# A decoder step on one core: VectorE takes each latent page apart four half pages ahead of its key products, in place of five

## The reference, cut to what matters

```
def page_block(phys):
    kn, kr, v = mla_keys(cache_l[phys], w_uk, w_uv, k_norm_nope)   # kn = rms_norm(c @ w_uk), 8 heads of 128
    return partial_softmax(mla_scores(qn, qr, kn, kr), v)
m_p, l_p, a_p = lax.map(page_block, page_table.T)
```

## Time and profile before

| | us |
|---|---|
| median of 3 runs | 1407.22 (1404.19 to 1407.71) |
| the profiled execution | 1408.25 |
| its span, first to last instruction | 1406.5 |
| PE busy in the span | 1381.6 (98%) |
| DVE, ACT, POOL busy | 1015.2, 857.7, 292.9 |
| page loop, about 95 to 1065 on PE | 970 for 128 pages |

### The profile page before, as it was taken

One profiled execution on the slowest core, in us unless ns is written; L12 is line 12 of the kernel. 1 busy time (PEld: TensorE's weight loads), 2 busy tenths in 40 slices (PEclk: granted clock), 3 DMA queues, 4 the chain that ended last, 5 costly groups with the idle time before them and its releaser, 6 DMA issues.

```text
span 1406.5 us, 30025 instructions
## 1 busy us (share of the span) xinstructions
PE 1381.6 (98%) x9428; PEld 1168.5 (83%) x9428; DVE 1015.2 (72%) x3674; ACT 857.7 (61%) x2780; POOL 292.9 (21%) x339
## 2 busy tenths in 40 slices
PE   9999999999999999999999999999999999999998
PEld 7877887887778777778877888778778999999998
DVE  5766667788777886877887777778765567777543
ACT  5445788687666686575866666865783453444332
POOL 3012312222422222331322322322331000000000
PEclk9999999999999999999999999999999999999999
DMA  9442326753445544356543564444564565555551
GB/s 282 126 119 51 80 48 147 166 123 76 95 111 146 119 114 80 72 127 158 124 99 84 113 130 99 86 98 87 113 165 160 169 240 164 167 180 180 181 182 58
DMA packets 282890, 180.05 MB, mean 128 GB/s; under 512 B 183072, under 2 KB 229696, under 8 KB 282728
## 3 DMA queue, kind: packets, MB, share of 16 engines
q1 hardware_dynamic: 282418, 177.86, 49.5%
q10 hardware_dynamic: 318, 0.33, 0.1%
HBM read 134.32 MB, written 6.77 MB: 100 GB/s over the span
## 4 chain that ended last, share of the span: by engine, by line
PE 81%; DVE 7%; ACT 6%; issue 3%; SPq 2%; DMA 1%; POOL 0%; DVEq 0%; ACTq 0%
PE ps L2067 14%; PE ps L2069 13%; PE ps L2068 13%; PE ps L2471 6%; PE ps L2472 6%; PE ps L2473 6%; PE ps L2089 2%; ACT ksq L895 2%; PE ps L2142 2%; PE ps L2419 2%; PE ps L2420 2%; PE ps L2421 2%; PE ps L2143 2%; PE ps L2144 2%; DVE prod L1285 1%
## 5 line engine op out<-in xcount | busy, mean ns | idle before, releaser
L2067 PE MATMUL ps<-ukh,cTh 128*128 128x512 f32 x1024 | 416.6, 407 | 8.8 <-DVE sparts L1285 7.1
L895 ACT ACTIVATE ksq<-ps 128x128 f32<-128x128 f32 x1024 | 268.1, 277 | 235.8 <-PE ps L2069 235.1
L2068 PE MATMUL ps<-ukl,cTh 128*128 128x512 f32 x1024 | 400.9, 392 | 0.0
L2069 PE MATMUL ps<-ukh,cTl 128*128 128x512 f32 x1024 | 400.9, 392 | 0.0
L1285 DVE CUSTOM_DVE_ANT_0 prod<-ps,qb 128x128 f32<-128x128 f32 x1024 | 234.0, 284 | 23.8 <-ACT ksq L895 19.3
L2067 PEld LDWEIGHTS ps<-ukh,cTh 128*128 128x128 f32 x1024 | 193.3, 189 | 63.5 <-issue 25.2
L2069 PEld LDWEIGHTS ps<-ukh,cTl 128*128 128x128 f32 x1024 | 192.8, 188 | 42.7
L2068 PEld LDWEIGHTS ps<-ukl,cTh 128*128 128x128 f32 x1024 | 193.2, 189 | 34.1
L747 POOL TENSOR_TENSOR rk<-kss,mhalf 128x8 f32<-128x8 f32 x128 | 217.5, 1699 | 10.7
L895 ACT ACTIVATION_READ_ACCUMULATOR ksq<-ps 128x1 f32 x1024 | 212.6, 208 | 0.0
L882 ACT ACTIVATE cTr<-turned 128x1024 uint16<-128x1024 uint16 x126 | 174.8, 1387 | 2.4 <-DMA turned<-planes 2.3
(11 more groups left out here) (504 smaller groups left out, 2701.1 us busy)
## 6 DMA issues: line engine op xcount, KB each, us to landing
clat<-cache_mla SPq DMA_DIRECT2D x128, 256.0 KB, 2.6
wraw<-w_in SPq DMA_DIRECT2D x16, 1024.0 KB, 5.1
wraw<-w_up SPq DMA_DIRECT2D x16, 1024.0 KB, 5.4
wraw<-w_down SPq DMA_DIRECT2D x16, 1024.0 KB, 5.0
braw<-w_in SPq DMA_DIRECT2D x24, 512.0 KB, 4.5
crope<-cache_mla SPq DMA_DIRECT2D x128, 32.0 KB, 2.4
qb<-scratch SPq DMA_DIRECT2D x16, 256.0 KB, 3.7
sst<-state_gdn SPq DMA_DIRECT2D x32, 128.0 KB, 3.1
```

Source lines behind the costliest of these rows:

```text
L895: i = nc.scalar.activation(ksq[m % 3], ps[:, k % 3, P * h:P * h + P], ACT.Square, accum_out=kss[:, n // 4 % 2, n % 4, h0 + h:h0 + h + 1]). ...
L2067: mm(out, cTh[:, n % 2, c], ukh[:, c, cols], start=c == 0, stop=False)
L2068: mm(out, cTh[:, n % 2, c], ukl[:, c, cols], start=False, stop=False)
L2069: i = mm(out, cTl[:, n % 2, c], ukh[:, c, cols], start=False, stop=c == 3)
```

## The change

DVE's `split_planes` moves from behind `beside(2n+1)` to behind `split_lo(n+1)`, and takes page `n+2` in place of `n+3` there. A page is so taken apart one iteration later less the steps between the two places: four half pages ahead of its key products, where it was five. No instruction is added or taken out.

```
                     scored(n - 1, 1)
                 if n + 1 < NT:
                     split_lo(n + 1)
+                if n and n + 2 < NT:
+                    split_planes(n + 2)
                 if t == 1 and g >= 1:
                     scaled(g - 1)
...
                 beside(2 * n + 1)
-                if n + 3 < NT:
-                    split_planes(n + 3)
                 if n:
                     scored(n, 0)
```

## The result

The changed kernel takes **1468.52 us** (median of 4 runs, 1463.84 to 1470.35) where the kernel before takes 1407.47 (1404.19 to 1407.81): a ratio of 1.0435, with a 95% interval of 1.0415 to 1.0455. It is slower by 61 us. The direction was forecast, but the size was not: 16.6 us were forecast, and the range ended at 1438. The profiled execution took 1463.84 us, with a span of 1462.1 us. So what the trace shows (1462.1 - 1406.5 = 55.6 us more) is a little less than the difference of the medians.

The account below looks back on a forecast made before the run. PE, busy 98% of the span, was taken as the bound. Terms of 9.5 + 3.1 + 5.0 - 1.0 = +16.6 us gave 1423.8 us; forecast 1413 to 1432 (67%), range 1409 to 1438.

Parts of the forecast that it names:

- The ring: Page loop: landed, cTr, cTh, cTl, copy, issue on SP, landed; no page follows its predecessor in less than 6.7 us.
- four such stretches: Around pages 26, 52, 67 and 102, ACT works without pause and a late landing delays everything; 1.25 us each.
- The closing pages: Pages 119 to 127 ran at 5.84 us each, under the ring's length: +9.5 us, bounds +3.1 and 18.5.
- The projections: Pairs 1 and 3: the copy now precedes bwl, which ends 0.61 us later: +3.1 us, bounds 0 and 6.1.
- The other tight pages: Four loop stretches where ACT has no pause and late landings delay everything: +5 us, bounds 0 and 12.
- the forecast's last sentence: Wrong if closing pages stay under 6 us, landings get much quicker, or PE's waits grow at unnamed places.
- The gain: DVE's waits for a landing before the copy vanish, mostly without cost to PE before: -1.0 us, bounds 0 and -3.
- Covered: Rival: ACT's waits for PE in the loop absorb late landings; 1407 to 1411 us; 14%.
- faster: Rival: DVE scores banks sooner, so PE's 7.1 us of waits for them go; 1401 to 1403 us; 4%.
- SP snowballs: Rival: 25 group loads on SP's queue each add 1.3 us to the ring; 1433 to 1445 us; 15%.

Follow-up runs that it names:

- the loads two and two: The kernel before, SP's four page loads of a group split into two and two around its first page's transposition: 1406.37 us, ratio 1.0003.
- opening the ring: The changed kernel with the copy two pages ahead put in front of the next page's low half: 1424.28 us; 1431.18 on another chip.
- the kernel without a ring: The changed kernel copying three pages ahead (six half pages), each group's first-page copy left at its old place: 1419.01 us, ratio 1.0091.
- The six-half-page run: The changed kernel with its copy at the new place taking the page three ahead instead of two: 1445.97 us, ratio 1.0279.

## Why the prediction was right in its sign and wrong in its size

**The ring** was right, with its length. The transpositions of the changed kernel stand 6.66 us apart where nothing else is in the way (499.11 to 505.77), and 6.7 was worked out. That shortening it, lengthening it and opening it all move the time, and that the same edits move the kernel before little or not at all, is shown by the runs.

**The step that failed** is: "in long pages the ring has time to spare, and it gives back lateness there", together with "I see some four such stretches", 1.25 us each. The ring was set against the loop's mean of 7.6 us a page. But the pages are not turned at their mean. In the kernel before, one in four comes 9.5 us after its predecessor, and the other three come at 6.9 to make up for it. SP's loads in between are half of the reason: with the loads two and two it is still 8.6, against 7.2. The rest is probably DVE's softmax steps (`scaled`, `probabilities`, `accumulate`), which it does once a group between these two copies; no run shows it. Against 6.7 the three pages have 0.2 us each to spare. Even that is too much: 6.7 was reckoned with the median landing, 3.2 us, but the landings of the changed kernel have a mean of 3.39, with one in four over 3.5 and the longest 6.3, and wherever the ring is the bound it pays them. With the mean it is 6.9, and nothing is left. The issues could no longer bunch as before (6.9 became 7.5), and the mean went from 7.57 to 8.02 us: (1047.2 - 101.1)/125 by the earlier trace rows, against (1103.5 - 101.1)/125 by

```profile
L534 SPq DMA_TRANSPOSE turned<-planes x126: 1232/1237/2617, 101.1 to 1103.5; - x126
```

0.45 us for each of 125 steps, 56 us in all. Splitting the loads gives 24 us back and opening the ring 37 to 44, which bears this out. With both, 55 of the 61 us are gone.

Where PE lost them is to be seen page by page, from the start of each page's first product against the kernel before. It is 0.5 us late at page 26, 4.7 at 28, 5.8 at 42, 13.1 at 48, 18.9 at 54, 29.3 at 93, 34.1 at 99, 39.7 at 119 and 55.6 at 127 (1113.05 against 1057.47). The four stretches that were named (26 to 28, 50 to 54, 67 to 68, 102 to 104) make 12.1 us of it, where 5 were put. From 42 to 48 and from 93 to 99, where pairs 1 and 3 make their projections, it is 12.1 as well. These are pages of 9 to 10 us, the long ones in which lateness was to be given back. 3.4 of these 12.1 us are the clock (the two stretches from 436.80 and 471.00).

**The closing pages** were forecast at +9.5 us (3.1 to 18.5). `cTl` of page 119, 120 and 127 in the changed kernel:

```profile
1047.86 0.68 DVE L1273 TENSOR_TENSOR cTl<-cTr,cTh 128x512 fp32r<-128x512 f32 x1
...
1050.32 0.69 DVE L1261 COPY planes<-clat 128x1024 uint16<-128x1024 uint16 x1 [1.78 <-DMA crope<-cache_mla]
...
1058.94 0.69 DVE L1273 TENSOR_TENSOR cTl<-cTr,cTh 128x512 fp32r<-128x512 f32 x1 [5.24 <-ACT cTh L885]
...
1108.88 0.69 DVE L1273 TENSOR_TENSOR cTl<-cTr,cTh 128x512 fp32r<-128x512 f32 x1
```

From 119 to 127 it is 61.0 us where 46.75 were the earlier trace rows, +14.3. From first product to first product on PE, as the term was reckoned, it is +15.8 (64.0 where 48.1 were), within the bounds. Nothing behind the loop gave it back, as forecast. The seven rounds took 49.9 us, and 48.9 were worked out (7 x 6.7 and 1.95). Most of the rest is the step to page 120, 11.1 us, since the copy for page 120 came at 1050.32 only, after 1.78 us of waiting for the page itself, and SP's state writes and page loads held the transposition until 1053.28. But page 119 was already 1047.86 - 1008.15 = 39.7 us late, where the other terms gave 7.1. Nearly all that was missed arose in the body of the loop.

**The projections** (+3.1) hold for what they priced: the wait for `bwl` went from 3.2 to 6.2 us, and the kernel without a ring has it too. The pages around them lost more, as said.

**The other tight pages** (+5, bounds 0 to 12) is the term that failed in size: what the terms for the projections, the tight pages and the gain had to cover came to 39.7 us. Two parts of it were counted nowhere. One is the pair steps held up behind `cTl`. I had put the late landing on ACT and on the page alone. On DVE it stops everything behind it, and PE's new waits for `qkv`, `X_`, `oT`, `Xc` and their like are what the forecast's last sentence named as the sign that it would be wrong. The other is the clock: 9.4 us of PE time at 1.2 GHz, of which the sum had none.

**The gain** (-1.0): DVE's wait for landings before the copy is gone, as forecast, and no gain is to be seen. It turned up one instruction earlier: `cTl`'s wait grew by 79.5 us.

**The rivals.** "Covered" and "faster" are out. "SP snowballs" had the right mechanism (the loads meet a ring with no spare time) and was still too small with its 12 to 20 us, since it too let the projection pages clear the lateness. The six-half-page run shows a further bound that I hadn't seen: the copy can't come much earlier either, as the page isn't there yet. The old place lies between the two.

No version here beats the kernel before. The kernel before with its loads two and two is the same (ratio 1.0003).

Left open: how the 12.5 us of the run without a ring divide between the steps held up by the copy and DVE's longer waits for the planes to be read.

## What to carry to other kernels

When a change closes a ring, set the ring's length against the shortest spacing that the loop needs to catch up, not against its mean: one slow step in four, here a group's first page with SP's loads ahead of it, uses up what the mean seems to leave. Reckon the ring with the mean of its transfers, not with their median, where they have a long tail. Then list what is queued behind each wait of the ring on its in-order engine, work of other streams included, as that is where the bound engine starts to wait. A producer has a place that is too early (its input hasn't arrived) and one that is too late (its own successor waits); swapping two neighbouring instructions across the wait was worth 40 us here.

## What the runs showed of the hardware

- A transposing DMA of 128x1024 two-byte numbers lands 3.2 us after its issue at the median (mean 3.39 in the changed kernel and 3.55 in the kernel before), one of 128x512 2.4 us, and SP is held for 1.24 and 1.19 us by them: half the bytes save a quarter of the time to landing and almost nothing of the issue.
- In the changed kernel's loop, four of the eight waits of PE of 2.0 to 3.0 us were followed by a stretch at 1.2 GHz, and four were not, the longest (3.04 us) among them. What is sure is the sum: PE's busy time for the same matmuls was 1381.6, 1397.1, 1419.9 and 1447.4 us at spans of 1406.5, 1462.1, 1536.0 and 1593.0 us, with mean granted clocks of 0.995, 0.988, 0.974 and 0.961. 28 to 35% of what the last three lose against the first is PE busy for longer with the same work.
